# Two weight groups' low parts on GpSimd, and new step lists for both mixers

## The reference

```
block 1:  h = rms_norm(x);  qa ka va qb kb vb f g = h @ w_in           (1024 x 5128)
          8 heads of block attention with RoPE (qa ka va), 8 heads with forgetting (qb kb vb, f)
          x += (gate0 * o_a @ w_branch_moba + gate1 * o_b @ w_branch_fox) @ w_out
          u g = rms_norm(x) @ w_ffn_up; x += (silu(conv(g)) * u) @ w_ffn_down
block 2:  h = rms_norm(x);  hq hf hi hg sq sk sv iq ik iw mq = h @ w_in_2   (1024 x 3656)
          a gated linear recurrence (HGRN: q, f, i, g), 4 heads of attention over the 64 keys that an
          indexer chooses (iq, ik, iw; sq, sk, sv), 4 heads over a memory (mq; mk, mv from mem_2)
          x += [hgrn, sparse, memory] @ w_out_2;  x += (silu(g) * u) @ w_ffn_out_2
```

## Time and profile before

| | |
|---|---|
| median of the runs | 734.34 us (733.11 to 734.57) |
| the profiled execution | 732.7 us, its span 730.9 us |
| TensorE busy | 716.3 us (98%) |
| VectorE busy | 511.1 us (70%) |
| ScalarE busy | 451.9 us (62%) |
| GpSimd busy | 8.4 us (1%) |
| granted TensorE clock, mean | 0.997 |

### The profile page before, as it was taken

The page is one execution under the profiler, slowest core; times in us unless marked ns, Lnnn a source line. Parts: engine busy times, 40 slices in busy tenths (PEclk is TensorE's granted clock), DMA queues, the critical chain, the costliest instruction groups (busy, mean ns, idle before and its releaser), DMA issues.

```text
span 730.9 us, 11816 instructions
## 1 busy us (share of the span) xinstructions
PE 716.3 (98%) x4460; PEld 617.0 (84%) x4460; DVE 511.1 (70%) x792; ACT 451.9 (62%) x694; POOL 8.4 (1%) x18
## 2 busy tenths in 40 slices
...
GB/s 333 239 273 125 241 145 159 130 146 158 160 144 195 180 175 206 193 175 202 255 214 177 124 169 86 127 113 145 69 192 215 242 188 155 169 209 217 228 102 30
DMA packets 70463, 127.95 MB, mean 175 GB/s; under 512 B 4915, under 2 KB 17172, under 8 KB 70420
## 3 DMA queue, kind: packets, MB, share of 16 engines
...
HBM read 126.30 MB, written 1.05 MB: 174 GB/s over the span
## 4 chain that ended last, share of the span: by engine, by line
PE 81%; ACT 7%; DVE 6%; DMA 4%; issue 2%; SPq 1%; ACTq 0%; DVEq 0%
PE acc L607 19%; PE acc L609 18%; PE acc L608 18%; PE acc L599 6%; PE acc L600 6%; PE acc L601 6%; DVE b_wlo L1562 2%; ACT b_whi L1069 2%; DMA b_raw<-in_w_in 1%; PE banks L629 1%; PE banks L642 1%; DMA b_gates<-in_mem 1%; PE banks L659 1%; DMA b_raw<-in_w_out 1%; DMA b_raw<-in_w_ffn_in 1%
## 5 line engine op out<-in xcount | busy, mean ns | idle before, releaser
L1562 DVE TENSOR_TENSOR b_wlo<-b_raw,b_whi 128x1024 fp32r<-128x1024 f32 (+4 forms) x232 | 269.0, 1187 | 97.3 <-ACT b_whi L1069 96.1
L1069 ACT ACTIVATE b_whi<-b_raw 128x1024 fp32r<-128x1024 f32 (+4 forms) x232 | 231.6, 1027 | 92.0 <-PE acc L609 30.9
L607 PE MATMUL acc<-b_whi,b_hhi 128*128 128x512 f32 (+4 forms) x480 | 186.1, 388 | 0.3 <-DVE b_hqT L2010 0.3
L609 PE MATMUL acc<-b_wlo,b_hhi 128*128 128x512 f32 (+4 forms) x480 | 181.0, 377 | 0.0
L608 PE MATMUL acc<-b_whi,b_hlo 128*128 128x512 f32 (+4 forms) x480 | 180.9, 377 | 0.0
L607 PEld LDWEIGHTS acc<-b_whi,b_hhi 128*128 128x128 f32 x480 | 90.2, 188 | 18.3 <-issue 2.5
L609 PEld LDWEIGHTS acc<-b_wlo,b_hhi 128*128 128x128 f32 x480 | 90.2, 188 | 14.9
L608 PEld LDWEIGHTS acc<-b_whi,b_hlo 128*128 128x128 f32 x480 | 90.3, 188 | 13.2
L599 PE MATMUL acc<-b_ohi,b_whi 128*128 128x256 f32 x352 | 99.9, 284 | 1.6 <-DVE b_olo L1595 1.5
L600 PE MATMUL acc<-b_olo,b_whi 128*128 128x256 f32 x352 | 99.6, 283 | 0.0
L601 PE MATMUL acc<-b_ohi,b_wlo 128*128 128x256 f32 x352 | 99.6, 283 | 0.0
...
## 6 DMA issues: line engine op xcount, KB each, us to landing
...
```

The lines of the kernel that those rows point to most:

```text
L607: nc.tensor.matmul(o, a, wh, start=first, stop=False)
L609: mm = nc.tensor.matmul(o, a, wl, start=False, stop=last)
L1069: ins = A(whi[:, n % SPLIT, 0:c["nk"], 0:c["n"]], raw[:, n % RAW, 0:c["nk"], 0:c["n"]], ACT.Copy)
L1562: ins = V.tensor_tensor(wlo[:, n % SPLIT, 0:c["nk"], 0:c["n"]], raw[:, n % RAW, 0:c["nk"], 0:c["n"]], whi[:, n % SPLIT, 0:c["nk"], 0:c["n" ...
```

## The change

1. `POOL_LOWS = ("sqk", "hg")`: the lows of these two groups' eight chunks (154 to 161) are made by GpSimd behind its RoPE, each when its high is ready, and counted by a semaphore of their own. VectorE leaves them out. `low_ready(n)` gives TensorE's and SP's waits the right semaphore and count.
2. `ORDER1` and `ORDER2` are laid out anew, for all three engines. The steps are the same, only their places change. Chunk order: va 1 goes behind ka 3 (before, it stood ahead of ka 2), and iqb 0 ahead of hq 3.

```diff
+POOL_LOWS = ("sqk", "hg")
...
+        by_pool = sorted(n for g in POOL_LOWS for n in groups[g]["at"])
+
+        def low_ready(n, i=0):
+
+            if n in by_pool:
+                return sem("late low ready"), by_pool.index(n) + 1
+            return sem("lo ready"), n + 1 + PER * i - sum(m < n for m in by_pool)
...
-                    pe.wait_ge(sem("lo ready"), n + 1 + PER * i)
+                    pe.wait_ge(*low_ready(n, i))
...
-                    sp.wait_ge(sem("lo ready"), n - RAW + 1)
+                    sp.wait_ge(*low_ready(n - RAW))
...
+                if n in by_pool:
+                    return
                 dve.wait_ge(sem("hi ready"), n + 1 + PER * i)
...
             rope("ka")
+            for n in by_pool:
+                c = chunks[n]
+                pool.wait_ge(sem("hi ready"), n + 1)
+                G.tensor_tensor(wlo[:, n % SPLIT, 0:c["nk"], 0:c["n"]], raw[:, n % RAW, 0:c["nk"], 0:c["n"]],
+                                whi[:, n % SPLIT, 0:c["nk"], 0:c["n"]].bitcast(F32), ALU.subtract)\
+                 .then_inc(sem("late low ready"), 1)
```

Of the lists, the places that the prediction speaks of (one engine's list in each line, `-` before, `+` after, cut):

```diff
 PE 1:  -("gemm","ka",1,0), ("gemm","va",0,0), ("gemm","ka",1,1), ("gemm","ka",2,0), ("gemm","va",0,1), ("gemm","va",1,0)
        +("gemm","ka",1,0), ("gemm","ka",2,0), ("gemm","va",0,0), ("gemm","va",1,0), ("gemm","ka",1,1), ("gemm","va",0,1)
 PE 1:  -("gemm","kb",3,0), ("gemm","kb",1,1), ("gemm","kb",2,1), ("probs",0), ("gemm","kb",3,1), ("scores",2), ("pv",0)
        +("gemm","kb",1,1), ("gemm","kb",3,0), ("probs",0), ("gemm","kb",2,1), ("gemm","kb",3,1), ("scores",2), ("pv",0)
 PE 1:  -("gemm","vb",1,0), ("probs",2), ("gemm","fg2",2,1), ("gemm","fg2",3,1), ("turn","kb"), ("gemm","vb",1,1), ("scores",4)
        +("gemm","vb",1,0), ("gemm","fg2",2,1), ("gemm","fg2",3,1), ("turn","kb"), ("gemm","vb",1,1), ("probs",2), ("scores",4)
 DVE 1: -("scores",0), ("lo","fg1",1), ("squares","qb"), ("scores",1), ("lo","fg2",0), ("divide",0), ("heads","qb")
        +("scores",0), ("lo","qb",3), ("lo","fg1",1), ("squares","qb"), ("lo","fg0",1), ("divide",0), ("scores",1), ("heads","qb")
 DVE 1: -("norm sum","ffn1",0,0), ("lo","wo1_1",3), ("norm gain","ffn1",0,0), ..., ("norm gain","ffn1",1,0), ("lo","s1",1),
         ("norm lo","ffn1",0,0), ("norm sum","ffn1",1,1), ("norm lo","ffn1",0,1), ...
        +("norm sum","ffn1",0,0), ("lo","s1",1), ("norm gain","ffn1",0,0), ..., ("norm gain","ffn1",1,0),
         ("norm lo","ffn1",0,0), ("norm lo","ffn1",0,1), ("norm sum","ffn1",1,1), ...
 ACT 1: -("hi","fg3",2), ("probs",2), ("turn","kb")      +("hi","fg3",2), ("turn","kb"), ("probs",2)
 DVE 2: -("sums","hf",0,1), ("log","hf"), ("sums","hq",0,1), ("lo","hi",2), ("log","hq")
        +("sums","hf",0,1), ("sums","hq",0,1), ("lo","hi",2), ("log","hq"), ("log","hf")
 PE 2:  -("level",2), ("gemm","hi",0,1), ("level",4), ("gemm","hi",3,0), ("gemm","hi",1,1), ("level",8)
        +("level",2), ("gemm","hi",0,1), ("gemm","hi",3,0), ("level",4), ("gemm","hi",1,1), ("level",8)
 ACT 2: -("turn","iq"), ("hi","sqk",3), ("sums","hi",0), ("index",0), ("hi","hf",1), ("index",1), ("place",32), ("sums","hi",1)
        +("sums","hi",0), ("sums","sviq",0,1), ("turn","iq"), ("hi","sqk",3), ("index",0), ("index",1), ("sums","hi",1)
 PE 2:  -("index",2), ("gemm","mq",1,1), ("gemm","sqk",1,0), ("gemm","mq",2,1), ("index",3), ("gemm","mq",3,1), ("level",128),
         ("gemm","sqk",0,1), ("hout",0)
        +("index",2), ("gemm","mq",1,1), ("gemm","mq",2,1), ("index",3), ("gemm","mq",3,1), ("level",128),
         ("gemm","sqk",0,1), ("gemm","sqk",1,0), ("hout",0)
 DVE 2: -("near",0), ("decay",32), ("lo","sqk",1), ("index",0), ("lo","d1_1",10), ("decay",64), ("index",1), ("index",2), ("decay",128)
        +("near",0), ("decay",32), ..., ("index",0), ("lo","hf",0), ("decay",64), ("index",1), ("index",2), ("decay",128)
 PE 2:  -("probs",8), ("gemm","hg",2,0), ("gemm","hg",0,1), ("pv",8)      +("probs",8), ("gemm","hg",0,1), ("pv",8)
 ACT 2: -("hi","wo2_0",0), ("turn","sqk"), ("hi","wo2_0",3), ("sums","hg",0,1)
        +("turn","sqk"), ("hi","wo2_0",0), ("sums","hg",0,1)
 ACT 2: -("norm hi","ffn2",0,1), ("hi","hi",0), ("norm squares","ffn2",0), ("norm hi","ffn2",1,0), ..., ("norm hi","ffn2",1,1)
        +("norm hi","ffn2",0,1), ("norm hi","ffn2",1,1), ("norm squares","ffn2",0), ("hi","hg",2), ("norm hi","ffn2",1,0), ...
```

More of the change, by code:

```diff
@@ L102 @@
[L102 to L110, removed]
+     ("turn", "ka"), ("gemm", "fg0", 1, 0), ("gemm", "fg0", 0, 1), ("scores", 0), ("gemm", "qb", 3, 1),
@@ L111 @@
+     ("turn", "qb"), ("gemm", "fg1", 3, 1), ("decay sums", 0), ("gemm", "fg2", 1, 0), ("gemm", "fg2", 2, 0),
+     ("gemm", "fg2", 3, 0), ("gemm", "fg2", 0, 1), ("gemm", "vb", 0), ("scores", 3), ("pv", 1), ("gemm", "fg2", 1, 1),
+     ("gemm", "vb", 1, 0), ("gemm", "fg2", 2, 1), ("gemm", "fg2", 3, 1), ("turn", "kb"), ("gemm", "vb", 1, 1),
+     ("probs", 2), ("scores", 4), ("pv", 2), ("gemm", "vb", 2, 0), ("probs", 3), ("gemm", "vb", 3, 0),
      ("gemm", "vb", 2, 1), ("scores", 5), ("pv", 3), ("gemm", "fg3", 0), ("gemm", "vb", 3, 1), ("gemm", "fg3", 1, 0),
@@ L191 @@
-     ("gemm", "mq", 1, 1), ("gemm", "sqk", 1, 0), ("gemm", "mq", 2, 1), ("index", 3), ("gemm", "mq", 3, 1),
-     ("level", 128), ("gemm", "sqk", 0, 1), ("hout", 0), ("gemm", "hg", 0, 0), ("turn", "mq"), ("hout", 1),
-     ("scores", 8), ("gemm", "sqk", 2, 0), ("gemm", "sqk", 1, 1), ("gemm", "sqk", 3, 0), ("scores", 9),
-     ("gemm", "sqk", 2, 1), ("gemm", "hg", 1, 0), ("gemm", "sqk", 3, 1), ("probs", 8), ("gemm", "hg", 2, 0),
-     ("gemm", "hg", 0, 1), ("pv", 8), ("gemm", "hg", 1, 1), ("probs", 9), ("pv", 9), ("gemm", "hg", 2, 1),
@@ L196 @@
-     ("turn", "sqk"), ("gemm", "hg", 3), ("scores", 10), ("gemm", "wo2_0", 3, 0), ("gemm", "wo2_0", 3, 1),
-     ("scores", 11), ("gemm", "wo2_1", 3), ("probs", 10), ("pv", 10), ("out", 2), ("out", 0), ("probs", 11),
-     ("pv", 11), ("gemm", "wo2_0", 0), ("gemm", "wo2_0", 1), ("gemm", "wo2_0", 2, 0), ("gemm", "wo2_1", 1, 0),
+     ("gemm", "hf", 3, 1), ("gemm", "iqb", 0, 0), ("gemm", "hq", 3, 0), ("gemm", "hq", 2, 1), ("gemm", "iqb", 0, 1),
+     ("gemm", "hq", 3, 1), ("gemm", "iqb", 1, 0), ("gemm", "iqb", 2, 0), ("gemm", "sviq", 0, 0),
@@ new lines @@
+     ("turn", "iq"), ("gemm", "mq", 0), ("gemm", "mq", 1, 0), ("gemm", "mq", 2, 0), ("index", 0),
+     ("gemm", "mq", 3, 0), ("level", 32), ("index", 1), ("gemm", "sqk", 0, 0), ("level", 64), ("index", 2),
+     ("gemm", "mq", 1, 1), ("gemm", "mq", 2, 1), ("index", 3), ("gemm", "mq", 3, 1), ("level", 128),
+     ("gemm", "sqk", 0, 1), ("gemm", "sqk", 1, 0), ("hout", 0), ("gemm", "hg", 0, 0), ("turn", "mq"), ("hout", 1),
+     ("scores", 8), ("gemm", "sqk", 2, 0), ("gemm", "sqk", 1, 1), ("gemm", "sqk", 3, 0), ("gemm", "sqk", 2, 1),
@@ new lines @@
+     ("scores", 9), ("gemm", "sqk", 3, 1), ("gemm", "hg", 1, 0), ("probs", 8), ("gemm", "hg", 0, 1), ("pv", 8),
+     ("gemm", "hg", 2, 0), ("gemm", "hg", 1, 1), ("probs", 9), ("pv", 9), ("gemm", "hg", 2, 1), ("turn", "sqk"),
+     ("gemm", "hg", 3), ("scores", 10), ("gemm", "wo2_0", 3, 0), ("gemm", "wo2_0", 3, 1), ("scores", 11),
+     ("gemm", "wo2_1", 3), ("probs", 10), ("pv", 10), ("out", 0), ("out", 2), ("probs", 11), ("pv", 11),
+     ("gemm", "wo2_0", 0), ("gemm", "wo2_0", 1), ("gemm", "wo2_0", 2, 0), ("gemm", "wo2_1", 1, 0),
@@ L203 @@
 ORDER2["act"] = [("hi", "hq", 0), ("norm hi", "x2", 0, 1), ("norm hi", "x2", 0, 0), ("hi", "hf", 3),
-     ("norm squares", "x2", 0), ("norm hi", "x2", 1, 0), ("norm squares", "x2", 1), ("norm guess", "x2"),
-     ("hi", "hq", 3), ("norm hi", "x2", 1, 1), ("hi", "iqb", 3), ("hi", "iqb", 2), ("rows", "x2"), ("log", "hf"),
-     ("hi", "iqb", 1), ("hi", "sviq", 2), ("log", "hq"), ("hi", "hi", 2), ("sums", "iqb", 0), ("exp", "q"),
-     ("exp", "k"), ("exp", "f"), ("hi", "hi", 3), ("sums", "iqb", 1), ("hi", "sqk", 0), ("sums", "sviq", 0, 1),
@@ L208 @@
-     ("turn", "iq"), ("hi", "sqk", 3), ("sums", "hi", 0), ("index", 0), ("hi", "hf", 1), ("index", 1), ("place", 32),
-     ("sums", "hi", 1), ("hi", "sviq", 1), ("hi", "hg", 0), ("index", 2), ("hi", "mq", 0), ("hi", "mq", 3),
-     ("sums", "mq", 0), ("place", 64), ("place", 0), ("place", 128), ("sums", "mq", 1), ("guess", "mq"), ("hout", 0),
-     ("index", 3), ("hi", "hg", 1), ("turn", "mq"), ("scores", 8), ("hi", "wo2_1", 3), ("divide", 8), ("hout", 1),
-     ("sums", "sqk", 0), ("probs", 8), ("scores", 9), ("sums", "sqk", 1), ("pv", 8), ("divide", 9), ("guess", "sqk"),
@@ L213 @@
-     ("probs", 9), ("hgrn squares", 0), ("gain", 0), ("hi", "mq", 2), ("hi", "hg", 3), ("hi", "mq", 1), ("pv", 9),
-     ("hi", "wo2_0", 0), ("turn", "sqk"), ("hi", "wo2_0", 3), ("sums", "hg", 0, 1), ("log", "hg"), ("scores", 10),
-     ("guess", "hgrn"), ("divide", 10), ("exp", "g"), ("probs", 10), ("scores", 11), ("hi", "hg", 2), ("pv", 10),
[4 rows of a table removed]
+     ("norm hi", "x2", 1, 0), ("norm squares", "x2", 0), ("norm squares", "x2", 1), ("norm guess", "x2"),
[4 rows of a table added]
```

(19 more changed lines are left out.)

74 lines of the change are left out of this document (45 added, 29 removed), and 81 rows, old and new, of the table pick.

## The result

| | before | after |
|---|---|---|
| median of the runs | 734.34 us (733.11 to 734.91, 5 runs) | 738.05 us (737.58 to 738.79, 5 runs) |
| the profiled execution | 732.7 us, span 730.9 | 737.98 us, span 736.2 |
| ratio | | 1.0054 (95% interval 1.004 to 1.0069) |

The change makes the kernel 3.7 us slower. The forecast was 733.7, 0.6 us faster, with a range up to 737.4: the sign and the size were wrong. What happened is rival B, GpSimd's lows between VectorE's instructions.

A forecast was written before the change was run, and what follows sets the result against it. TensorE's own stream was taken to bound the kernel. The terms -2.1 + 1.4 - 0.3 + 0.4 made -0.6 us, set against the median 734.34: 733.7 us, range 730.5 to 737.4.

The forecast's parts named there:

- rival B: Second mixer: GpSimd gets the lock between VectorE's instructions, 2.4 lows priced, +2.9 us, 737.2, at most 738.6; chance 0.22.
- Part 1: Eight lows leave VectorE, 9.8 us less there, but none ends a wait of TensorE: credit 0.
- Part 2: A low on GpSimd takes 2.5 us (bounds 1.22 and 3.6); late lows cost 0, up to 1 us.
- Part 3: Second mixer, 455 to 480: two-input instructions of GpSimd and VectorE shut each other out, once in that stretch: +1.4 us.
- Part 4: First mixer's new lists remove stalls before probs 0, scores 4 and s1: -2.1 us.
- Part 5: Rest of second mixer: hq's row scalings ahead of log hf -0.29; high wo2_0 0 +0.3, probs 8 +0.1.
- Rival C: No low is in the way and the half-clock stretch goes: -3.6 us, 730.7; chance 0.26.

The follow-up runs named there:

- e5: Changed kernel with all lows on VectorE, divide 8 ahead of three bests, lows of hg 2 and 3 behind them: 729.64 us, -3.2 against before.
- e11: Same kernel as e5, run again on another chip: 728.25 us, -5.0 against before.
- e6: Changed kernel, but GpSimd copies raw into wlo instead of subtracting (one SBUF input): 729.9 us, -3.0 against before.
- e10: Changed kernel, but GpSimd fills wlo with zeros instead of subtracting (no SBUF input): 729.12 us, -4.1 against before.
- e1: Changed kernel's lists for both mixers, all lows on VectorE, first two lows of sqk behind decay 32: 733.82 us, -1.2 against before.
- e9: The changed kernel, unchanged, run again on another chip: 737.42 us, +4.2 against before.
- e2: Lists of the kernel before for both mixers, lows of sqk and hg by GpSimd: 740.48 us, +5.5 against before.
- e3: Kernel before with the new lists for the first mixer alone, second mixer and lows as before: 732.55 us, -2.4 against before.
- The mended list: Second mixer's list of e5 with the first mixer's list of the kernel before: 732.49 us, -0.8 against before.
- e7: Changed kernel, but GpSimd makes only the four lows of hg, VectorE those of sqk: 730.8 us, -2.1 against before.

## Why the prediction was wrong, by its steps

**Part 1 (credit 0 for VectorE's relief): right.** e5 and e11, with all lows on VectorE, are as fast as e6 and e10, in which VectorE has none of those eight. The relief is worth something only under the new place of divide 8 (e1 -1.2 against e6 -3.0, each against its own group: 1.8 us), a place that needs it.

**Part 2 (a low on GpSimd 2.5 us, late lows 0): right.** 2.36 to 2.69; no wait of TensorE for a GpSimd low shows.

**Part 3 (the lock; "If GpSimd gets the lock once in that stretch"; +1.4): this step failed.** The mechanism was right, the number of times was not. I took once "because VectorE's instructions there stand close together, with one gap, of 1.07 us". The reading was incomplete and, worse, from the wrong kernel. VectorE's timeline of before at this place:

```profile
461.93 2.35 DVE L1562 TENSOR_TENSOR b_wlo<-b_raw,b_whi 128x1024 fp32r<-128x1024 f32 x2
464.97 0.55 DVE L2031 TENSOR_SCALAR b_spare<-b_spare,b_iw 128x256 f32<-128x256 f32 x2 [0.69 <-ACT b_spare L1498]
```

There is a second gap, of 0.69 us, ahead of index 0, and the two lows ahead of it fill the rest of the time in which VectorE waits for ScalarE's relu. The change takes these lows out, and so opens a gap of 2.66 us just where three highs become ready. GpSimd enters it with three lows in a row, and index 0's two short instructions get in one per low: 4.67 us instead of 0.55. Level 64, which was in no term, waits 3.38. The clock falls behind it, 1.57 (2.7 in e9); no term had that either. In place of the +1.4, this stretch lost 7.2 us. At level 16 decay 16 came when I had said (458.96; I had "some 459.0"), but TensorE was there 1.2 us earlier thanks to the gains ahead, so the stall was 1.84, not 0.6: these gains were given back at the first barrier whose other side had not moved. In e2, without them, the stall is 0.36. Rival B had the case and priced it at 737.2, at most 738.6; its 0.22 was too little. For the late stretch I had said that VectorE has mostly one-input instructions there: the TENSOR_SCALAR are held as well. The one of 1.60 is covered, the one of 0.98 costs 0.4 at turn mq.

The Trainium skill has this too ("SBUF — State Buffer", section Who interferes with whom: a VectorE tensor_scalar in its two-port mode contends with GpSimd, an instruction with two SBUF inputs only with a GpSimd instruction that reads SBUF). By the copy of e6 (0.63 and 1.53 us) and the fill of e10 (0.52 and 0.68), the runs agree, though no row says in which mode a TENSOR_SCALAR ran; I had used only its half on two inputs.

**Part 4 (first mixer, -2.1): right.** e3 gave -2.4, and the three brackets are gone. **Part 5 (-0.29 + 0.4): not refuted.** The mended list gives -0.8, with an interval (-1.6 to +0.4 us) that takes in the forecast +0.1. It did not price divide 8, which costs 3 us as soon as the lows of hg are VectorE's. In after that is nothing, so it is a miss of reading, not of the result.

**The sum** with the measured terms: -2.4 (first mixer) - 0.8 (second list) + 7.2 (level 16 to scores 8, clock and turn mq among it) = +4.0, against +3.7 and +4.2 measured. That it fits so well is in part luck: the -0.8 is not clear of noise, and with e9's 2.7 for the clock the sum is +5.1. Rival C's end of the half-clock stretch did come in after's profile (1.00 from 512 to 530, where the shifted work stands, against 0.91 from 507 to 525 before) and not in e9's (0.82), nor in e7's (0.81 from 507 to 525). Since after and e9 are one kernel, it goes by the execution; what decides it stays open.
